# RWKV-7 scan on one core: the transposed inverse by VectorE's 32x32 block transposition instead of TensorE's products

## The reference

```python
def rwkv7_scan(r, w, k, v, kk, a, s0):
    def step(s, inp):
        rt, wt, kt, vt, kkt, at = inp
        sa = jnp.einsum('nbhij,nbhj->nbhi', s, kkt)
        s = (s * wt[..., None, :] - sa[..., :, None] * (kkt * at)[..., None, :]
             + vt[..., :, None] * kt[..., None, :])
        return s, jnp.einsum('nbhij,nbhj->nbhi', s, rt)
```

## Time and profile before

| | |
|---|---|
| median of 3 runs | 4923.35 us (4911.92 to 4924.96) |
| profiled execution | 4895.91 us |
| its span | 4894.1 us, granted TensorE clock 0.951 of full speed |
| TensorE busy | 4312.2 us (88% of the span) |
| VectorE busy | 2182.8 us (45%) |
| ScalarE busy | 1217.1 us (25%) |
| GpSimd busy | 1545.0 us (32%) |
| stage of the scans | about 1471 to 2980 us from the start |

### The profile page before, as it was taken

How to read it: one execution, slowest core, us unless ns; L and a number is a source line. 1 busy time by engine, 2 the same in 40 slices (tenths; PEclk the granted TensorE clock), 3 DMA queues, 4 the chain that set the end, 5 groups by cost and what they waited for, 6 DMA issues and landing times. The chain is left out here.

```text
span 4894.1 us, 124383 instructions
## 1 busy us (share of the span) xinstructions
PE 4312.2 (88%) x47746; PEld 2948.8 (60%) x47746; DVE 2182.8 (45%) x4021; ACT 1217.1 (25%) x3134; POOL 1545.0 (32%) x1931
## 2 busy tenths in 40 slices
PE   2999979999978989888988895877699999998997
PEld 0777856667658888888888884444333333333333
DVE  1111156767756555555555554888311111111115
ACT  0000034444434343433333332332000000000000
POOL 0000001110116565665656563443422222221220
PEclk7999989999989999999999997988799999999999
DMA  9411155665642322222232324442675899999877
GB/s 291 175 64 55 46 155 187 202 209 184 205 160 78 98 77 85 83 75 88 76 98 77 98 76 145 143 139 95 252 309 223 356 389 395 388 395 417 330 287 292
DMA packets 321434, 917.01 MB, mean 187 GB/s; under 512 B 72528, under 2 KB 171216, under 8 KB 271600
## 3 DMA queue, kind: packets, MB, share of 16 engines
q1 hardware_dynamic: 266192, 759.98, 44.0%
q0 software_dynamic: 47328, 133.02, 7.5%
q10 hardware_dynamic: 7488, 17.83, 0.9%
HBM read 951.09 MB, written 211.26 MB: 238 GB/s over the span
## 5 line engine op out<-in xcount | busy, mean ns | idle before, releaser
L2490 PE MATMUL exp_gate_up<-exp_w_gate,exp_rows_and_rowsT 128*64 128x512 f32 x1664 | 739.9, 602 | 43.9 <-DMA exp_w_up<-in_moe_w_up_dram 42.9
L2490 PE MATMUL exp_gate_up<-exp_w_up,exp_rows_and_rowsT 128*64 128x512 f32 x1664 | 740.6, 602 | 0.0
L2490 PEld LDWEIGHTS exp_gate_up<-exp_w_gate,exp_rows_and_rowsT 128*64 128x64 f32 x1664 | 229.0, 139 | 528.1 <-issue 527.9
L1554 POOL TENSOR_TENSOR rw_A_level<-rw_A_rho_beta,const_level_masks 128x256 f32<-128x256 f32 x432 | 370.6, 877 | 459.8 <-DVE rw_A_rho_beta L1570 335.7
L721 PE MATMUL rwp_product<-rwp_hT,rwp_w_rw 128*128 128x256 f32 (+1 forms) x2016 | 443.5, 383 | 0.0
L721 PEld LDWEIGHTS rwp_product<-rwp_hT,rwp_w_rw 128*128 128x128 f32 (+1 forms) x2016 | 380.8, 189 | 60.9
L874 PE MATMUL hgp_product<-hgp_hT,const_w_hg 128*128 128x256 f32 x1728 | 393.7, 383 | 15.8 <-DMA hgp_hT<-s_hT 15.8
L2441 DVE TENSOR_TENSOR exp_hidden<-exp_hidden,exp_gate_up 64x512 f32<-64x512 f32 x104 | 71.9, 692 | 741.6 <-ACT exp_hidden L2422 741.6
L2515 PE MATMUL exp_down<-exp_w_down,exp_hiddenT 128*64 128x512 f32 x1664 | 380.0, 598 | 1.3
L874 PEld LDWEIGHTS hgp_product<-hgp_hT,const_w_hg 128*128 128x128 f32 x1728 | 326.6, 192 | 70.4 <-DMA hgp_hT<-s_hT 16.2
L1585 DVE TENSOR_TENSOR rw_inverse<-rw_inverse,rw_inverse_bank 128x512 f32<-128x512 f32 x288 | 196.9, 684 | 308.1 <-PE rw_inverse_bank L1464 307.4
(11 more groups left out here) (396 smaller groups left out, 7966.3 us busy)
## 6 DMA issues: line engine op xcount, KB each, us to landing
exp_w_gate<-in_moe_w_gate_dram SPq DMA_DIRECT2D x208, 1024.0 KB
exp_w_up<-in_moe_w_up_dram SPq DMA_DIRECT2D x208, 1024.0 KB
exp_w_down<-in_moe_w_down_dram SPq DMA_DIRECT2D x104, 2048.0 KB
s_rw_in<-prep_operands SPq DMA_DIRECT2D x72, 514.0 KB, 4.0
rw_operands<-s_rw_in SPq DMA_DIRECT2D x72, 514.0 KB, 4.9
rw_tokens<-s_rw_tm SPq DMA_DIRECT2D x144, 192.0 KB, 5.9
hg_qkf<-s_hg_in SPq DMA_DIRECT2D x36, 768.0 KB, 7.6
mod_w<-in_w_mod_dram SPq DMA_DIRECT2D x24, 1024.0 KB, 26.1
```

The costliest lines, as they stand in the source:

```text
L1554: nc.gpsimd.tensor_tensor(self.al[d][l % 2][:], self.ar[u][d][:, :, 0, :], self.K["lvc"][:, d, l, :].unsqueeze(1).broadcast_to([P, NPAIR, ...
L2490: i = nc.tensor.matmul(pgu[u][q:q + BLK], xT[:, k, r * BLK:(r + 1) * BLK], w[r][:, k, :], start=(k == 0), stop=(k == KD - 1))
```

## The change

The transposed half of `rt` is no longer kept by products. `turn` and its copy on ScalarE are gone, and so is the second set of products in `grow`. VectorE adds only the half that holds R, raises a new semaphore (`grown`), waits on it and transposes the 128x256 tile in blocks of 32x32 into the other half (`turned`). `cross` waits for that. `state` goes behind `cross4` in the order, `HG_GAPS` has other gaps (the first is now ahead of `cross1`, 3 items into the even step, and not ahead of `cross2`, 7 items in), and VectorE's list is sorted by its times.

```diff
--- before.py
+++ after.py
@@ -1306,7 +1306,7 @@
                 group_rounds(dve, body)
 
 
-RW_ORDER = ("gram0 rhs gram1 turn cross1 solve grow1 cross2 out grow2 cross3 grow3 state cross4 grow4 cross5 grow5").split()
+RW_ORDER = ("gram0 rhs gram1 cross1 solve grow1 cross2 out grow2 cross3 grow3 cross4 state grow4 cross5 grow5").split()
 
 
 def rw_time(name, d, later=0.0):
@@ -1333,7 +1333,7 @@
         self.st, self.rhs, self.uu, self.y = (one(x, [P, NPAIR, RW_C]) for x in ("state", "rhs", "u", "y"))
         self.pa = [m.ps(f"inverse_bank{d}", [P, 2, NPAIR, RW_C]) for d in range(2)]
         self.pb = [m.ps(f"chain_bank{d}", [P, 2, NPAIR, RW_C]) for d in range(2)]
-        names = ("grams masked level_ready r_ready t_psum t_ready x_psum x_ready rd_psum "
+        names = ("grams masked level_ready grown r_ready x_psum x_ready rd_psum "
                  "rhs_psum rhs_ready u_psum u_ready y_psum y_ready s_psum s_ready s_order y_stored").split()
         self.s = [{n: sem(f"{n}{d}") for n in names} for d in range(2)]
         self.loaded = two(lambda u, d: sem(f"loaded{u}{d}"))
@@ -1432,21 +1432,11 @@
                 i = nc.tensor.matmul(dst[q, j, :], left[q, j, :], both[q, :, j, :], start=True, stop=True)
             i.then_inc(s["grams"], 1)
 
-        def turn(d):
-            s = self.s[d]
-            pe.wait_ge(s["r_ready"], 6 * n + 1)
-            pe.wait_ge(s["masked"], 2 * n + 2)
-            pe.sem_inc(self.turns, 1)
-            for j, q in heads:
-                i = nc.tensor.matmul(self.pa[d][q, 1, j, :], self.rt[u][d][q, 0, j, :], K["idc"][q, :], start=True, stop=True)
-            i.then_inc(s["t_psum"], 1)
-
         def cross(d, l):
             s = self.s[d]
             if l == 1:
-                pe.wait_ge(s["t_ready"], n + 1)
-            else:
-                pe.wait_ge(s["r_ready"], 6 * n + l)
+                pe.wait_ge(s["masked"], 2 * n + 2)
+            pe.wait_ge(s["r_ready"], 6 * n + l)
             pe.wait_ge(s["level_ready"], 6 * n + l + 1)
             pe.sem_inc(self.turns, 1)
             for j, q in heads:
@@ -1459,9 +1449,6 @@
             pe.sem_inc(self.turns, 1)
             for j, q in heads:
                 i = nc.tensor.matmul(self.pa[d][q, 0, j, :], self.x[d][q, j, :], self.rt[u][d][q, 0, j, :], start=True, stop=True)
-            if l < 5:
-                for j, q in heads:
-                    i = nc.tensor.matmul(self.pa[d][q, 1, j, :], self.rt[u][d][q, 0, j, :], self.x[d][q, j, :], start=True, stop=True)
             i.then_inc(s["rd_psum"], 1)
 
         chain = {"rhs": rhs, "solve": solve, "out": out, "state": state}
@@ -1478,8 +1465,6 @@
                 if name in chain:
                     if not (isinstance(n, int) and n == 0):
                         chain[name](d)
-                elif name == "turn":
-                    turn(d)
                 else:
                     {"gram": gram, "cross": cross, "grow": grow}[name[:-1]](d, int(name[-1]))
 
@@ -1502,11 +1487,6 @@
             act.wait_ge(s["y_psum"], n)
             wait(act, s["y_stored"], 16 * (n - 1))
             nc.scalar.activation(self.y[d][:], self.pb[d][:, 0], ACT.Copy).then_inc(s["y_ready"], 1)
-
-        def turned(d):
-            s = self.s[d]
-            act.wait_ge(s["t_psum"], n + 1)
-            nc.scalar.activation(self.rt[u][d][:, 1], self.pa[d][:, 1], ACT.Copy).then_inc(s["t_ready"], 1)
 
         def crossed(d, l):
             s = self.s[d]
@@ -1524,9 +1504,6 @@
                 if name in chain and not (isinstance(n, int) and n == 0):
                     yield rw_time(name, d, 1.6)
                     chain[name](d)
-                elif name == "turn":
-                    yield rw_time(name, d, 1.6)
-                    turned(d)
                 elif name[:-1] == "cross":
                     yield rw_time(name, d, 1.6)
                     crossed(d, int(name[-1]))
@@ -1577,14 +1554,17 @@
                 dve.wait_ge(s["level_ready"], 6 * n + 1)
                 wait(dve, s["u_psum"], n - 1)
                 V.tensor_tensor(rt[:, 0], self.al[d][0][:], K["idc"][:].unsqueeze(1).broadcast_to([P, NPAIR, RW_C]), ALU.add)\
-                    .then_inc(s["r_ready"], 1)
+                    .then_inc(s["grown"], 1)
             else:
                 dve.wait_ge(s["rd_psum"], 5 * n + l)
                 dve.wait_ge(s["r_ready"], 6 * n + l)
-                if l < 5:
-                    V.tensor_tensor(rt[:], rt[:], self.pa[d][:], ALU.add).then_inc(s["r_ready"], 1)
-                else:
-                    V.tensor_tensor(rt[:, 0], rt[:, 0], self.pa[d][:, 0], ALU.add).then_inc(s["r_ready"], 1)
+                V.tensor_tensor(rt[:, 0], rt[:, 0], self.pa[d][:, 0], ALU.add).then_inc(s["grown" if l < 5 else "r_ready"], 1)
+
+        def turned(d, l):
+            s = self.s[d]
+            flat = lambda t: t.rearrange("p j t -> p (j t)")
+            dve.wait_ge(s["grown"], 5 * n + l + 1)
+            V.transpose(flat(self.rt[u][d][:, 1]), flat(self.rt[u][d][:, 0])).then_inc(s["r_ready"], 1)
 
         def state(d):
             s = self.s[d]
@@ -1599,15 +1579,18 @@
             state(0)
             state(1)
             return
-        steps = [("gram0", 1.6, lambda d: mask(d, 0)), ("gram0", 3.7, lambda d: inverse(d, 0)), ("gram1", 1.6, lambda d: mask(d, 1))]
-        steps += [(f"grow{l}", 1.6, lambda d, l=l: inverse(d, l)) for l in range(1, 4)]
+        steps = [("gram0", 1.6, lambda d: mask(d, 0)), ("gram0", 3.7, lambda d: inverse(d, 0)), ("gram0", 3.8, lambda d: turned(d, 0)),
+                 ("gram1", 1.6, lambda d: mask(d, 1))]
+        for l in range(1, 6):
+            steps.append((f"grow{l}", 1.6, lambda d, l=l: inverse(d, l)))
+            if l < 5:
+                steps.append((f"grow{l}", 1.7, lambda d, l=l: turned(d, l)))
         if not (isinstance(n, int) and n == 0):
-            steps += [("state", 1.6, state)]
-        steps += [(f"grow{l}", 1.6, lambda d, l=l: inverse(d, l)) for l in range(4, 6)]
-        for name, later, f in steps:
-            for d in range(2):
-                yield rw_time(name, d, later)
-                f(d)
+            steps.append(("state", 1.6, state))
+        timed = sorted(((rw_time(name, d, later), d, f) for name, later, f in steps for d in range(2)), key=lambda x: x[0])
+        for time, d, f in timed:
+            yield time
+            f(d)
 
 
 def rw_gap(step, name):
@@ -1615,8 +1598,8 @@
     return 0.5 * (step + RW_ORDER.index(name) / len(RW_ORDER))
 
 
-HG_GAPS = ([rw_gap(0, x) for x in "cross2 cross3 grow3 grow4 cross5 grow5".split()]
-           + [rw_gap(1, x) for x in "rhs turn cross1 cross2 grow2 cross3 grow3 grow4 cross5 grow5".split()])
+HG_GAPS = ([rw_gap(0, x) for x in "cross1 cross2 cross3 grow3 cross4 cross5 grow5".split()]
+           + [rw_gap(1, x) for x in "gram0 cross1 cross2 cross3 grow3 cross4 cross5 grow5".split()] + [0.99])
 HG_AT = [(0.0, HG_GAPS[0] - 0.10), (0.09, HG_GAPS[0] - 0.01)] + [(hg_time(t), g) for t, g in enumerate(HG_GAPS)] + [(HG_OUT, 1.0), (2.0, 2.1)]
```

## The result

The changed kernel takes 5063.85 us (median of 4 runs, 5059.71 to 5068.74) against 4924.16 us of the kernel before in the same rounds (4 runs, 4911.92 to 4929.94): ratio 1.0287, interval 1.0269 to 1.0304. It is slower by 140 us; the prediction said 4930 and a range up to 5020. The profiled execution took 5059.7 us against 4895.9 before, 163.8 more, and that difference is what the rows can explain.

What follows compares the result with a forecast made beforehand. TensorE's own list of work was taken as the bound. Per pair, -9.3 + 4.0 + 5.4 + 3.1 - 2.8 = +0.4 us, 17 times: +7 us, giving 4930 us on the median, range 4835 to 5020.

Steps and rivals of the forecast that it cites:

- at a full clock: First reading of the scan stage: TensorE busy 449.5 us in 500 at a full clock, its list of work the bound.
- Late instructions: TensorE's "issue" waits: fewer instructions and more places to catch up take 2.8 us a pair off, bounds 0.7 and 6.4.
- Load of the odd step: TensorE's wait for the odd step's load after the state update grows to 4.9 us, 3.1 a pair on.
- Front: Start of the even step: HGRN2's work, moved ahead, delays masks and cross1; net 5.4 us a pair on.
- level to level: From growing products to the next cross: VectorE's add and transposition open holes in TensorE, 4.0 us a pair on.
- The transposition, 0.44: VectorE's new block transposition between levels, taken as 0.44 us because it has one SBUF input.
- The rival that priced it at 0.93: Slower: a 0.93 us transposition on VectorE sets every level's clock, +6 a pair, +102 us, 5030; chance 0.23.
- Products removed: TensorE in the scans: 360 groups of `turn` and second growing products at 0.467 us go, 9.3 us a pair off.
- given back: Whole kernel: holes return what removed products save, net within 3 us a pair, 4870 to 4990; chance 0.50.

Runs made afterwards that it cites:

- e9: e2 plus 2 and 4 unread products ahead of cross1 of the even step; 4858.87 us, 0.9905 of the kernel before.
- e12: e2 with HGRN2's first sums behind both masks, plus 3 and 1 unread products ahead of cross2 of the even step; 4840.28 us, ratio 0.9875.
- e5: Changed kernel plus 7 and 4 unread 128x256 products ahead of cross1 of the two directions; 4973.01 us, 1.0131 of the kernel before.
- e8: e2 with the second growing products of levels 1 to 4 issued again but not read; 4913.34 us, 1.0004 of the kernel before.
- e6: e2 with HGRN2's load queued ahead of the RWKV load; 4902.75 us, 1.0001 of the kernel before.
- e7: e1 with `state` put back ahead of cross4; 4924.39 us, 1.0037 of the kernel before.
- e1: Changed kernel with HGRN2's work ahead of its first score task put back late, as in the kernel before; 4967.32 us, ratio 1.0132.
- e3: Kernel before with only HGRN2's front moved early, as in the changed kernel, all products kept; 4968.27 us, 1.0130 of the kernel before.
- e2: e7 with the old gaps and the front at cross2: the block transposition in the old order; 4882.51 us, 0.9950 of the kernel before.
- e4: Changed kernel plus 12 and 8 unread 128x256 products ahead of cross1 of the two directions; 5057.39 us, 1.0318 of the kernel before.

## Why the prediction was wrong, point by point

**The step that failed** is in its first view: "at a full clock". No term of the sum lets the clock change, and no reason is given for it, while 0.99 belonged to a TensorE that was busy 449.5 us in 500. The terms that open holes of 7.8 and 3.1 us a pair were the place to ask it again. It came to +5.8 us a pair, where the whole miss is 9.0. The trace puts over half of it behind the fronts and the load, and the rest behind "issue" waits. e9 and e12 show it by adding work and losing time, as e5 does for two thirds of its gain; e8 agrees.

**Late instructions, -2.8 a pair: wrong in sign.** "Issue" went from 5.3 to 8.1 us a pair with 12% fewer instructions in the pair. Against the 2.8 taken off that is an error of 5.6, as large as the clock's. That holes would absorb them was a guess from a count; the bound of 0.7 to 6.4 excluded a loss without a reason. The count did lower the waits with no transfer beside them, by 0.8 a pair; those beside transfers grew by 3.6. Why the instructions come later there stays open: e6 moved one suspect without effect, e8 has more instructions and still 15.2 us in place of 28.0 at L448, and e5 has fewer such waits than the changed kernel. The Trainium skill (Runtime: NRT & Kernel Launch, Instruction fetch mechanics) calls the cost of passing from one block of fetched instructions to the next mostly hidden. The traces here differ: 44 waits of over 1 us follow the 205 blocks of the changed kernel, and 46 the 269 of the kernel before.

**Load of the odd step, +3.1: right in direction, wrong in its parts.** A wait near 4.9 us a pair was said, and the row of the load shows 1.7, 0.7 more than before. In 7 of the 15 pairs the odd step's first products also wait for instructions (21.7 us, none before), which with the row makes +2.1. The place of `state`, said to be 0.93 of the 3.1, is worth 2.7 in e7. The rest was to come from the removed products alone, but in e7, which removes them too, the load's row is 0.2 a pair against 1.1 before. The term's sum of TensorE's work also names `state` without a figure; the parts that have one make the 6.5.

**Front, +5.4: held in size.** In the pair shown gram1 starts 5.3 us behind gram0 (6.0 said), cross1 at 11.5 (10.7 said, for GpSimd's level, where it was VectorE's mask) and, for the second direction, 14.5 (14.5 said); e1 prices its place at 4.5 a pair, e3 at 3.8 in the kernel before. By waits, front and levels together are +9.3 where the prediction had +9.4, so **level to level** (4.0 said, 2.4 by its row) was a little large and the front a little small.

**The transposition, 0.44: exact** (0.445). The estimate of 444 ns that the prediction works out from the page agrees with the 445 measured. The advice to keep the count of VectorE's operations low, which it quotes with it, stands in the Trainium skill (VectorE: DVE Perf Modes) in the section Rules for kernel authors, not in the one on the DRAIN. The rival that priced it at 0.93 is refuted, though the time went even beyond that rival's 5030.

**Products removed, -9.3:** right as work on TensorE, but no gain where nothing else fills its place; e8 prices the 7.5 of them that it brings back at 1.5.

Clock and "issue" aside, the measured terms add up to +0.8 a pair, and the prediction's, without its 2.8, to +3.2. So "given back" described the work and the holes, with the load priced 2.4 too high, which hid as much of the miss. The other two, one not asked for (+5.8) and one credited with the wrong sign (+2.8 in place of -2.8), make the rest: 5.8 + 5.6 - 2.4 = 9.0.

## What to carry to other kernels

When a change takes work off an engine that is nearly full, price the holes twice: their length, and the products behind them at the halved clock, for as long as a row of the profile at 0.50 shows. Make one change of the mathematics at a time with the order of the queues held fixed; here the transposition was worth 0.5% (e2), and the order rewritten around it cost 3.4%: the place of the front, of `state`, and the gaps, 76, 47 and 43 us. When a profile shows long "issue" waits, look for packets of its "instruction" queue just ahead of their ends, and for what else the DMA engines carry then. If a hole can't be closed, unread products just shorter than it pay, and products longer than it (e4) do not.

## What was not expected of the hardware

Adding 11 unread products a pair (3.29 and 1.99 us by e5's timeline) made the changed kernel 1.5% faster. Waits as short as 3.62 and 2.35 us with 0.68 us of work between them were followed by a granted clock of 0.50, and in the whole stretch of 1380 us TensorE was at half clock for 235.6 us against 20.5 before. And "issue" waits of up to 4.5 us stand in the middle of groups of products, longer than any wait for another engine in the same stretch: waits for instructions, which in the changed kernel exceed 1.9 us only while other transfers keep the DMA engines at least 30% busy.
